# A four-layer trunk on one core: where the attention's projection pieces, its chunk mask and the expert loads stand in their queues

## What is computed

```python
for q0 in range(0, s, Q_BLOCK):                     # 4 query blocks of 128
    q1 = q0 + Q_BLOCK
    sc = jnp.einsum("bhqd,bhkd->bhqk", qb, kb).astype(f32) * scale
    mask = (kpos[None, :] // CHUNK) <= (qpos[:, None] // CHUNK)     # CHUNK = 64
    p = jax.nn.softmax(jnp.where(mask, sc, -jnp.inf), axis=-1)
    a = p[:, :, 0] - lam * p[:, :, 1]
    outs.append(jnp.einsum("bhqk,bhkd->bhqd", a.astype(v.dtype), vb))
o = rmsnorm(jnp.concatenate(outs, axis=2), sub_norm) * (1.0 - lambda_init)
x = x + o @ w_o
...
logits = xf @ w_router                              # 8 experts
top_logit, top_idx = lax.top_k(logits, TOP_K)       # TOP_K = 2
gates = jax.nn.softmax(top_logit, axis=-1)
... each expert: (silu(x @ w_gate) * (x @ w_up)) @ w_down, F = 2816
```

## Time and profile before

| | us |
|---|---|
| median of 3 runs | 1925.56 (1925.25 to 1925.7) |
| profiled execution, its own time | 1926.86 |
| its span, first to last instruction | 1925.1 |
| PE busy | 1900.1 (99% of the span) |
| DVE, ACT, POOL busy | 813.2, 718.6, 549.1 |

### The profile page before, as it was taken

How to read it: one execution, slowest core, us unless ns; L and a number is a source line. 1 busy time by engine, 2 the same in 40 slices (tenths; PEclk the granted TensorE clock), 3 DMA queues, 4 the chain that set the end, 5 groups by cost and what they waited for, 6 DMA issues and landing times.

```text
span 1925.1 us, 29386 instructions
## 1 busy us (share of the span) xinstructions
PE 1900.1 (99%) x11978; PEld 1642.5 (85%) x11978; DVE 813.2 (42%) x1240; ACT 718.6 (37%) x1124; POOL 549.1 (29%) x296
## 2 busy tenths in 40 slices
PE   9999999999999999999999999999999999999998
PEld 7888788888888887877679999999999877888887
DVE  6465552200000007866741110110101676999997
ACT  5332232332222225366630000010010565878785
POOL 4466664365445544432221002010010100201010
PEclk9999999999999999999999999999999999999999
DMA  9523233233333232311109998888887787999993
GB/s 343 183 77 99 66 99 99 77 110 98 99 99 96 96 102 83 93 55 34 55 31 401 363 334 319 289 302 296 320 301 267 271 285 264 411 408 392 376 392 148
DMA packets 283561, 396.21 MB, mean 206 GB/s; under 512 B 12736, under 2 KB 190912, under 8 KB 283424
## 3 DMA queue, kind: packets, MB, share of 16 engines
q1 hardware_dynamic: 279488, 381.67, 56.6%
q0 software_dynamic: 3936, 12.62, 1.6%
HBM read 374.48 MB, written 21.08 MB: 205 GB/s over the span
## 4 chain that ended last, share of the span: by engine, by line
PE 95%; DVE 2%; ACT 1%; DMA 1%; issue 1%; DVEq 0%; SPq 0%; ACTq 0%; POOLq 0%
PE ps L2169 16%; PE ps L2176 8%; PE ps L2233 6%; PE ps L2235 6%; PE ps L2234 6%; PE ps L421 6%; PE ps L422 6%; PE ps L423 6%; PE ps L439 3%; PE ps L441 3%; PE ps L440 3%; PE ps L568 2%; PE ps L570 2%; PE ps L569 2%; PE ps L456 1%; PE ps L457 1%
## 5 line engine op out<-in xcount | busy, mean ns | idle before, releaser
L1296 POOL TENSOR_TENSOR w_lo<-raw,w_hi 128x1024 fp32r<-128x1024 f32 (+1 forms) x157 | 380.6, 2434 | 353.7 <-ACT w_hi L996 353.5
L2026 DVE TENSOR_TENSOR s_lo<-s_raw,s_hi 128x1024 fp32r<-128x1024 f32 x264 | 318.9, 1248 | 44.0 <-ACT s_hi L2430 36.3
L2430 ACT ACTIVATE s_hi<-s_raw 128x1024 fp32r<-128x1024 f32 x264 | 273.1, 1061 | 70.1 <-PE ps L2235 45.4
L996 ACT ACTIVATE w_hi<-raw 128x1024 fp32r<-128x1024 f32 x158 | 163.6, 1044 | 188.1 <-PE ps L441 115.6
L2774 DVE TENSOR_TENSOR hid<-ps,silu_g 128x160 f32<-128x160 f32 x88 | 28.6, 325 | 412.8 <-ACT silu_g L2390 412.7
L421 PE MATMUL ps<-act_a_hi,w_hi 128*128 128x512 f32 x512 | 199.6, 390 | 0.0
L422 PE MATMUL ps<-act_a_lo,w_hi 128*128 128x512 f32 x512 | 199.3, 389 | 0.0
L423 PE MATMUL ps<-act_a_hi,w_lo 128*128 128x512 f32 x512 | 199.2, 389 | 0.0
L2390 ACT ACTIVATE silu_g<-ps 128x160 f32<-128x160 f32 x88 | 26.9, 305 | 450.4 <-PE ps L2169 441.8
L2553 POOL TENSOR_TENSOR sum_rows<-sum_rows,y_rows_sb 128x1024 f32<-128x1024 f32 (+1 forms) x12 | 28.5, 2377 | 576.7 <-ACT y_rows_sb L2395 320.3
L2169 PE MATMUL ps<-xT,w_gate 128*128 128x132 f32 x1408 | 173.2, 276 | 2.8 <-DMA w_up<-in_moe_w_up 1.7
(11 more groups left out here) (458 smaller groups left out, 3173.1 us busy)
## 6 DMA issues: line engine op xcount, KB each, us to landing
w_gate<-in_moe_w_gate SPq DMA_DIRECT2D x44, 1024.0 KB, 5.3
w_up<-in_moe_w_up SPq DMA_DIRECT2D x44, 1024.0 KB, 8.6
w_down<-in_moe_w_down SPq DMA_DIRECT2D x44, 1024.0 KB, 10.6
s_raw<-in_moe_w_gate SPq DMA_DIRECT2D x44, 1024.0 KB, 8.1
s_raw<-in_moe_w_up SPq DMA_DIRECT2D x44, 1024.0 KB, 8.1
s_raw<-in_moe_w_down SPq DMA_DIRECT2D x44, 1024.0 KB, 7.4
raw<-in_even_w_in SPq DMA_DIRECT2D x42, 512.0 KB, 3.8
raw<-in_attn_w_qkv SPq DMA_DIRECT2D x24, 512.0 KB, 3.7
```

The costliest lines, as they stand in the source:

```text
L996: act.activation(w_hi[:, u % HL_SLOTS, 0:size(u)], raw[:, u % RAW_SLOTS, 0:size(u)], ACT.Copy).then_inc(hi_done, 1)
L1296: pool.tensor_tensor(w_lo[:, u % HL_SLOTS, 0:size(u)], raw[:, u % RAW_SLOTS, 0:size(u)], flat(w_hi[:, u % HL_SLOTS, 0:size(u)]), ALU.subtr ...
L2026: return eng.tensor_tensor(s_lo[u % S_HL][:], s_raw[u // 2 % S_RAW][:, u % 2, :], s_hi[u % S_HL][:].bitcast(F32), ALU.subtract)
L2430: act.activation(s_hi[u % S_HL][:], s_raw[q % S_RAW][:, u % 2, :], ACT.Copy).then_inc(s_high, 1)
```

## The change

Five edits:

1. The mask matmuls go. DVE writes the masked value into the corner before it takes the minimum, with a drain between.
2. `out_piece(j, 0)` and `out_piece(j, 2)` move from the end of a step, behind `heads`, to the place behind the scores, where piece 1 and 3 stand already.
3. `norm_o(0, 0)` moves on DVE from step 22 to step 20.
4. On DVE the router's `best_two(1)` moves behind the last `add_tile`, `best_two(2)` behind `keep_logits(3)`, its parts interleaved with tile 3's; the two small operations of the gates move from ahead of the rank count to behind the picks; each pick releases PE by itself, and PE gathers bank by bank, tile by tile.
5. SP issues a round's `w_down` behind the next round's `w_gate` and `w_up`.

```diff
 def scores(n):
-    pe.matmul(ps[:, b, 0:w], qT[r, pair, i * P:(i + 1) * P], kT[r, pair, 0:w],
-              start=True, stop=False, skip_group_check=True)
-    mm = pe.matmul(ps[:, b, w - 64:w], mask[r, 0:P], mask[r, P:P + 64],
-                   start=False, stop=True, skip_group_check=True)
+    mm = pe.matmul(ps[:, b, 0:w], qT[r, pair, i * P:(i + 1) * P], kT[r, pair, 0:w], start=True, stop=True)
...
             if j >= 1 and at == 0:
                 out_piece(j - 1, 3, 0)
+            if 0 <= j < NT and at in (1, 3):
+                out_piece(j, at - 1, 0)
             if n < N + 2:
                 turn_diff(n - 2)
             if n >= 3:
                 heads(n - 3)
-            if 0 <= j < NT:
-                if at == 1:
-                    out_piece(j, 0, 0)
-                if at == 3:
-                    out_piece(j, 2, 0)
...
 def least_scores(n):
     dve.wait_ge(scores_done, n + 1)
+    dve.memset(ps[0:64, score_bank(n):score_bank(n) + 2, P * i + 64:P * i + P], MASKED)
+    dve.drain()
     dve.tensor_reduce(soft[:, n % 4, 0:2], ps[:, score_bank(n):score_bank(n) + 2, 0:P * (i + 1)], AX.X, ALU.min
...
             k, after = divmod(n - O_STEP + 1, 4)
-            if 0 <= k < NT and after in (0, 2):
+            if n == 20:
+                norm_o(0, 0)
+            if 0 <= k < NT and (after == 2 or after == 0 and k):
                 norm_o(k, after // 2)
...
         best_two(0)
-        best_two(1)
         dve.memset(rt[:, 296:304], 1.0)
         dve.tensor_scalar(rt[:, 632:640], iota_e, -1.0, float(E - 1), ALU.mult, ALU.add)
         dve.wait_ge(unit_used, N_UNITS)
         add_tile(G_WO + 1, 3, 512)
+        best_two(1)
         keep_logits(2)
...
-                load_expert_round(sp, e, r, u % WSLOTS)
+                load_expert_hidden(sp, e, r, u % WSLOTS)
+                if r:
+                    load_expert_down(sp, e, r - 1, (u - 1) % WSLOTS)
+                if r == ROUNDS - 1:
+                    load_expert_down(sp, e, r, u % WSLOTS)
...
         pe.wait_ge(h_made, NT)
-        pe.wait_ge(routing, PICK_MADE)
-        for k in range(KD):
+        for bank in range(3):
             for tt in range(NT):
+                if bank == 0:
+                    pe.wait_ge(picks_made, tt + 1)
+                for k in range(3 * bank, min(3 * bank + 3, KD)):
...
-        top3 = tops.rearrange("p (t k) -> p t k", t=NT)
-        dve.tensor_tensor(gdiff[:, 0:4].unsqueeze(2), top3[:, :, 1:2], top3[:, :, 0:1], ALU.subtract)
-        dve.drain()
-        dve.tensor_tensor(gdiff[:, 0:4], gdiff[:, 0:4], moe_ss[:, 4:8], ALU.mult).then_inc(gate_diff, 1)
         dve.wait_ge(ranked, 1)
```

More of the change, by code:

```diff
@@ L320, in build_trunk, with load_expert_hidden, load_expert_down @@
     same_expert = rt[:, 600:608]
-    def load_expert_round(sp, e, r, s):
+    def load_expert_hidden(sp, e, r, s):
         wg, wu, wd = w_slots[s]
         c = slice(2 * P * r, 2 * P * (r + 1))
-        for dst, src, there in ((wg, t["moe_w_gate"][0][e, :, c], gate_in[s]), (wu, t["moe_w_up"][0][e, :, c], up_in[s]),
-                                (wd, t["moe_w_down"][0][e, c, :], down_in[s])):
+        for dst, src, there in ((wg, t["moe_w_gate"][0][e, :, c], gate_in[s]), (wu, t["moe_w_up"][0][e, :, c], up_in[s])):
             sp.dma_start(dst[:], src.rearrange("(k p) n -> p k n", p=P)).then_inc(there, 16)
+    def load_expert_down(sp, e, r, s):
+        sp.dma_start(w_slots[s][2][:], t["moe_w_down"][0][e, 2 * P * r:2 * P * (r + 1), :].rearrange("(k p) n -> p k n", p=P)
+                     ).then_inc(down_in[s], 16)
     def norm_h(dve, tt):
@@ L1717, in _ @@
         dve.tensor_scalar(stat[:, 61:62], head_ss[:, 36:37], -LAMBDA_INIT, None, ALU.add)
-        dve.memset(mask[:], 0.0)
-        dve.drain()
-        for r in (0, 64):
-            dve.memset(mask[r:r + 1, 0:64], MASKED)
-            dve.memset(mask[r:r + 1, P:P + 64], 1.0)
         for g in range(4):
@@ L1825, in moe_norm, with lg, best, back_logits @@
             norm_h(dve, tt)
+        def lg(tt):
+            return rt[:, 16 + 8 * tt:24 + 8 * tt]
+        def best(tt):
+            return rt[:, 48 + 8 * tt:56 + 8 * tt]
+        def back_logits(tt):
+            dve.wait_ge(routed, tt + 1)
+            dve.tensor_copy(lg(tt), ps[:, tt, 2 * P:2 * P + E])
+            dve.drain()
         def best_two(tt):
-            lg, best = rt[:, 16 + 8 * tt:24 + 8 * tt], rt[:, 48 + 8 * tt:56 + 8 * tt]
-            dve.wait_ge(routed, tt + 1)
-            dve.tensor_copy(lg, ps[:, tt, 2 * P:2 * P + E])
+            back_logits(tt)
+            dve.max(best(tt), lg(tt))
             dve.drain()
-            dve.max(best, lg)
-            dve.drain()
-            dve.max_index(top_i[:, tt, :], best, lg)
+            dve.max_index(top_i[:, tt, :], best(tt), lg(tt))
         def keep_logits(tt):
@@ L1865, in _ @@
         dve.tensor_copy(hT[:, 4:KD, 3 * P:4 * P], ps[:, 7, :].rearrange("p (a b) -> p a b", a=4)).then_inc(hT_last, 1)
-        best_two(2)
         keep_logits(3)
-        best_two(3)
+        back_logits(2)
+        dve.max(best(2), lg(2))
+        back_logits(3)
+        dve.max(best(3), lg(3))
+        dve.max_index(top_i[:, 2, :], best(2), lg(2))
+        dve.drain()
+        dve.max_index(top_i[:, 3, :], best(3), lg(3))
     return dict(block=block, acc_evac=acc_evac, soft_end=scratch + 65536 + 1024, h_tok=h_tok, h_made=h_made, norm_h=norm_h, moe_ss=moe_ss, scratch=scratch, x_sb=x_sb, sem=sem, place=place, ps=ps, gain=gain, gain_in=gain_in, ident=ident, ones=ones,
                 t_incl=t_incl, stat=stat, w_slots=w_slots, gate_in=gate_in, up_in=up_in, down_in=down_in,
-                rt=rt, idx=idx, top_i=top_i, pass_t=pass_t, load_expert_round=load_expert_round,
+                rt=rt, idx=idx, top_i=top_i, pass_t=pass_t, load_expert_hidden=load_expert_hidden,
+                load_expert_down=load_expert_down,
                 t_moe=(t["moe_w_gate"][0], t["moe_w_up"][0], t["moe_w_down"][0]))
 def build_experts(nc, out, h_slots, acc_evac, soft_end, x_sb, sem, place, ps, gain, gain_in, ident, ones, t_incl, stat,
-                  w_slots, gate_in, up_in, down_in, rt, idx, top_i, pass_t, load_expert_round,
+                  w_slots, gate_in, up_in, down_in, rt, idx, top_i, pass_t, load_expert_hidden, load_expert_down,
                   block, h_tok, h_made, norm_h, moe_ss, scratch, t_moe):
```

25 lines of the change are left out of this document (13 added, 12 removed).

## The result

| | before | after |
|---|---|---|
| median | 1925.67 us (1925.25 to 1926.36, 20 runs) | 1928.64 us (1925.54 to 1930.44, 20 runs) |
| span of the profiled execution | 1925.1 us | 1927.6 us |

The ratio is 1.0013, with a 95% interval of 1.0007 to 1.0019: slower, by 3.0 us of the medians, where 1923.5 was forecast and 1925.6 was the upper end of the range. By the prediction's own threshold of 3.9 us that is no change, its likeliest outcome, but it lies outside its range and has the other sign. The runs of the changed kernel are spread over 4.9 us, those of before over 1.1 us, and the spread goes with the mean granted TensorE clock of a run (1 is 2.4 GHz throughout): the five runs at 0.999 took 1925.54 to 1926.1, the five at 0.998 1927.3 to 1928.39, the ten at 0.997 1928.88 to 1930.44. The profiled execution is one of the last kind.

The account below looks back on a forecast made before the run. PE's own work and waits were taken to bound the kernel (95% of the chain). Masks -2.4, pieces +4.0, router and loads -3.4 sum to -1.8 us, 1923.8 on the median, put at 1923.5; range 1920.0 to 1925.6.

Parts of the forecast that it names:

- prediction's own threshold of 3.9 us: Whole kernel: about 0.2% is what a measurement tells from no change; faster means below 1921.7 us.
- masks -2.4: Attention up to step 22: dropping PE's mask matmuls frees 0.13 us for each of 18 items, -2.4 us.
- pieces +4.0: Attention from step 23: moved pieces wait for later inputs; loop passes with memset, plus 1.95 us at the tail, +4.0 us.
- router and loads -3.4: Router and experts' start: DVE's reorder -0.8 us, expert loads -2.6 us more.
- The memset, 0.25 us a step: DVE's masking write with drain takes 0.25 us (bounds 0.13 to 0.42), hidden up to step 22, on the loop after.
- the prediction's other estimate: DVE's memset into PSUM: the skill's errata table would make it 0.26 us, 0.34 a step with the drain.
- the collision stays: Step 22: POOL's w_lo starts 0.05 us ahead of DVE's diff, so diff is still held up; no gain booked.
- The wait of round 4: Experts, round 4: PE's 0.77 us idle was read as waiting for the transfers' end, and would go.
- The pieces fill the waits: Rival, attention from step 23: low parts come in time, +4.0 becomes -2, 1917.8 us; half gives 1920.8; chance 0.15.
- A collision goes away: Rival, step 22: diff starts 0.1 us ahead of POOL's w_lo, 1.7 us go, 1921.8 us; chance 0.2.
- `diff` of step 22 at 0.5 us: Sign, DVE in step 22: diff taking 0.5 us would show the prediction wrong.
- Slower: Rival, steps ahead of 23: DVE's memset at 0.42 us, colliding with POOL's w_lo, sets the pace, 1932.0 us; chance 0.05.

Follow-up runs that it names:

- e7: The kernel before with only the router's new order and picks (edit 4) and the experts' load order (edit 5): 1922.97 us.
- e12: The kernel before with edits 3, 4 and 5, and POOL's four w_lo gated to start behind set DVE operations: 1919.03 us.
- e13: The kernel before with edits 1, 3, 4 and 5, and POOL's four w_lo gated behind set DVE operations: 1921.45 us.
- e15: The changed kernel, all five edits, with POOL's four w_lo gated behind set DVE operations: 1924.21 us.
- e10: The kernel before with four of POOL's w_lo cut to 64 columns, that part of the product left out: 1923.07 us.
- e9: The kernel before with edit 1 alone and four of POOL's w_lo cut to 64 columns, that part of the product left out: 1924.33 us.
- e1: The changed kernel with 12 small fp32 matmuls put into each of PE's two long waits, steps 26 and 32: 1926.64 us.
- e3: The kernel before with edit 2 alone, the moved pieces: 1929.95 us.
- e16: The kernel before with edits 2 to 5, and POOL's four w_lo gated behind set DVE operations: 1922.44 us.
- e2: The changed kernel with edit 2 undone, the pieces behind heads again: 1923.82 us.
- e5: The kernel before with edit 1 alone and two of POOL's w_lo cut to 64 columns, that part of the product left out: 1928.88 us.
- e4: The kernel before with edit 1 alone, masks by DVE's memset: 1929.12 us.
- e14_fetch_shift: e13 with 32 small matmuls of 8 columns put on PE at its start: 1933.32 us.

## Why the prediction was wrong

The sum had three terms: masks -2.4, pieces +4.0 (some 0.9 of it the memset: four passes of the loop at 0.22), router and loads -3.4. Adding the edits in an order that has a kernel for each step gives what was measured:

| step | forecast, us | measured, us | from |
|---|---|---|---|
| edits 4 and 5 | -3.4 | -3.3 | e7 |
| collisions away, edit 3 in | (0) | -3.4 | e12 less e7 |
| edit 1: masks, memset | -2.4 + 0.9 | +2.4 | e13 less e12 |
| edit 2: pieces | +3.1 | +2.5 | e15's seven runs at 0.999 less e13 |
| collisions back | (0) | +2.0 | changed kernel's five runs at 0.999 less those of e15 |
| half clock | 0 | +2.8 | all 20 runs against these five |
| all | -1.8 | +3.0 | |

- **Masks, "18 x 0.13 = 2.4": the step that failed, with the memset behind it.** The masks' place was read from their start to the next piece's start, and all of it booked as freed. In the rows shown it measured 0.04 us an item, and 0.46 us in all (0.49 in the changed kernel), with 0.25 us given back at step 7. What fills the rest of the place without a mask is 0.09 us by which the piece starts late behind the scores' 64-row matmuls; from which cause, no run separated.
- **The memset, 0.25 us a step: its size was right** (0.24; its own 0.17 us is well under the 0.26 of the prediction's other estimate), and so was that it is hidden up to step 22. Behind it, edit 1 costs 1.5 us (`e10` to `e9`) and 1.7 (`e12` to `e13`) with the collisions away, where about 0.9 had been booked.
- **The first `w_up`: a term that wasn't there.** Edit 1 costs another 1.2 us at the first hidden tile, beside the fetches of a shorter PE program. In the changed kernel it took back the router's part: DVE's and PE's steps came sooner (the first load is issued 41.2 us behind the attention's last `turn_o`, not 42.2), the transfer 1.06 us later (9.08 us from issue to first hidden tile, not 8.02).
- **Half clock wasn't in the sum: the other step that failed.** The text forecast waits (for `add_out`, for `lo_ev`) but priced them by their length alone. Behind waits of 1.52 to 2.27 us the matmuls of the profiled executions took 0.43 us and not 0.23 for 3 to 4 us, at 1.7 us a time. It makes the difference between +0.2 and +3.0 (2.8 us; 2.1 by `e1`).
- **The collisions: "the collision stays" failed, but their own price didn't rise.** The one of step 22 vanished, and PE reached `scores(24)` 1.2 us sooner than before, counted from `scores(0)`; then `diff(23)` and `diff(24)` met two others, and PE lost 2.1 us from `scores(26)` to `scores(27)` against before, half clock included. "POOL first by 0.05 us" was wrong: `diff` came first by 0.23 us. I looked at the collision at hand and not at the next `w_lo` of the same series. Yet before had paid for its collisions too, 2.7 us (`e10`) to 3.4 (`e12` less `e7`), and at full clock the changed kernel pays 2.0. The 4.6 us that `e15` takes off hold the clock besides; against before's 3.4 they are 1.2 us of the loss.
- **Pieces: right in mechanism, and in size at full clock.** Less the memset's share +3.1 had been booked; it measured +2.8 alone (`e3` at 0.999), +2.5 and +3.2 in the gated pairs (the runs of `e15` and `e16` at 0.999). That `e3`'s median came out at +4.1, beside the +4.0, is luck: half clock made up for the memset that `e3` doesn't have. In detail the loop from step 23 was overrated (+2.15 forecast, +1.0 between `e12` and `e16`), and the tail from `scores(31)` to `turn_o(3, 0)` grew by 3.5 (14.5 to 18.0 us), where +1.95 was forecast; about 1.5 of it is half clock (granted clock 0.69 from 950 to 955 in `e16`). The idle in front of `turn_o(3, 0)` was there, 1.04 us.
- **Router and loads, -3.4: right** without edit 1 (`e7`, -3.3), in both parts (-1.0 and -2.3). In the changed kernel the loads' part came out: from the first hidden tile on the profiled execution gained 3.5 us, 2.8 of it waits of PE that are gone (1.7 and 1.1). The wait of round 4 was a transfer, as read.
- **The rivals.** "The pieces fill the waits" is dead in four settings. "A collision goes away" came in part, by the sign that the prediction had named against itself (`diff` of step 22 at 0.5 us), and didn't make the kernel faster. "Slower" named the right engine pair, with a collision in it, but at the wrong place (ahead of step 22) and at 0.05: that other collisions come, and that a wait brings half clock, should have been rivals of their own.

## What to carry to other kernels

Where two engines hold each other up by overlap (here a two-input SBUF operation of DVE that starts under a `w_lo` of POOL), price a change of a few tenths of a us by every pair of the loop behind it, not by the pair at hand, and better tie the one engine's start to the other's: four waits on POOL, with `norm_o(0, 0)` moved, gave 3.4 us. Price such collisions in the kernel before as well, or their whole cost is blamed on the change. Where a change makes a wait of PE as long as those here, ask for the price at half clock behind it. A moved piece fills a wait only if its own input is there sooner than what the wait is for. And what an instruction frees is the difference from neighbour to neighbour with and without it; here the profile of before alone didn't show it, as the rows of the matmuls change from 64 to 128 at that place.

## What the runs showed of the hardware

- DVE's two-input SBUF operation (`diff`, 0.48 us alone) that starts 0.04 to 2.1 us behind POOL's `w_lo` ends 0.3 to 0.4 us behind POOL's end; one that starts 0.01 us ahead waits as long (2.66 us); one 0.10 us ahead doesn't wait (0.48 us at 915.39, before). One-input operations (0.27 us at 912.40) and those with an operand in PSUM ran at their usual length under `w_lo`: the minimum (0.69 at 911.56, changed kernel), the memset (0.17 at 911.32), the low parts (0.75 at 917.14, before).
- A memset of 64 partitions x 128 float32 into PSUM takes 0.17 us, as in SBUF, and 0.24 with its drain.
- Waits of PE of 1.52 us (with 0.46 more behind it, `e2`), 1.65 (with 0.57, `e5`), 1.92 (`e3`, `e16`), 2.15 and 2.27 (changed kernel) were followed by the 1.2 GHz level. The same waits as in `e5`, 1.65 and 0.57 us, were followed by full clock in the profiled execution of `e4`, and among the runs of one kernel both mean clocks occur.
- Small float32 matmuls at the start of the program are slow: 32 of 8 columns took 13.7 us in `e14_fetch_shift`, 0.43 us each, where 12 of 128 columns took 2.6 us in the attention (`e1_fill`). Why wasn't tried.
- With a 16 KB and an 8 KB instruction fetch among them, the first two 1 MB transfers were there about 1.2 us later (9.08 to 9.24 us from first issue to first hidden tile, 7.91 to 8.03 without), with the 8 KB one alone 0.6 to 0.7 later. How a fetch holds them up no run shows.
